# Layer 0's expert tiles: rows stored by one transfer from 32 partitions, rows loaded as two halves

## The reference, cut to what matters

```python
h2 = rms_norm(x, norm2_g) * (1 + sc2) + sh2      # 512 x 1024
gates = top 2 of the best group of 4 experts, per token
for e in range(16):                              # w_gate, w_up: 1024 x 512; w_down: 512 x 1024
    a = silu(h @ w_gate[e]) * (h @ w_up[e])
    out = out + gates[:, e:e + 1] * (a @ w_down[e])
```

## Time and profile before

| what | value |
|---|---|
| runs, us | 980.45, 981.01, 983.0 |
| profiled execution, span, us | 981.6 |
| TensorE busy, share of the span | 85% |
| VectorE / ScalarE / GpSimd busy | 41% / 16% / 15% |
| mean granted clock of TensorE | 0.928 |
| moved by DMA | 322.56 MB, mean 329 GB/s |

### The profile page before, as it was taken

One profiled execution on the slowest core, in us unless ns is written; L12 is line 12 of the kernel. 1 busy time (PEld: TensorE's weight loads), 2 busy tenths in 40 slices (PEclk: granted clock), 3 DMA queues, 4 the chain that ended last, 5 costly groups with the idle time before them and its releaser, 6 DMA issues.

```text
span 981.6 us, 22337 instructions
## 1 busy us (share of the span) xinstructions
PE 830.5 (85%) x8859; PEld 485.7 (49%) x8859; DVE 406.2 (41%) x893; ACT 159.5 (16%) x384; POOL 151.3 (15%) x284
## 2 busy tenths in 40 slices
PE   4699999888996889999896671999887899998674
PEld 2236633555444446657463441587544455654332
DVE  2132722676545423333231124641834655553223
ACT  3201100454013011111010011311512000000001
POOL 2302100001402334433231234000000000000000
PEclk9799999999997799999997886899998899999778
DMA  9999997534998899999999995296076799999995
GB/s 355 348 390 374 349 366 285 230 100 163 382 413 311 338 343 398 391 397 385 384 394 402 399 381 199 89 340 257 1 290 256 293 419 420 420 419 399 418 412 235
DMA packets 82359, 322.56 MB, mean 329 GB/s; under 512 B 10688, under 2 KB 28320, under 8 KB 57712
## 3 DMA queue, kind: packets, MB, share of 16 engines
q1 hardware_dynamic: 62544, 288.42, 75.3%
q0 software_dynamic: 12160, 27.89, 8.0%
q10 hardware_dynamic: 7584, 5.19, 1.8%
HBM read 297.27 MB, written 24.28 MB: 328 GB/s over the span
## 4 chain that ended last, share of the span: by engine, by line
DMA 46%; PE 41%; DVE 7%; issue 3%; ACT 2%; POOL 1%; SPq 0%; DVEq 0%; POOLq 0%; ACTq 0%
DMA weight_ring<-in_w_up_dram 19%; DMA weight_ring<-in_w_gate_dram 18%; PE bank2to L1374 9%; DMA weight_ring<-in_w_mod_dram 5%; PE bank2to L1252 5%; PE bank L1255 4%; PE bank2to L1255 4%; PE bank L1465 4%; PE bank L1252 4%; PE bank2to L1155 2%; DVE score_max L1791 2%; DMA weight_ring<-in_w_in_dram 1%; DMA h_by_expert<-q_k_transposed,slot_numbers 1%; PE bank L1477 1%; PE bank L1327 1%
## 5 line engine op out<-in xcount | busy, mean ns | idle before, releaser
L1465 PE MATMUL bank<-weight_ring,qk_tokens 128*32 128x256 f32 x3824 | 250.9, 406 | 59.5 <-DMA weight_ring<-in_w_up_dram 54.3
L1465 PEld LDWEIGHTS bank<-weight_ring,qk_tokens 128*32 128x32 f32 x3824 | 145.2, 116 | 147.4 <-issue 86.3
L881 POOL DMA_DIRECT2D qk_tokens<-h_by_expert x144 | 71.6, 497 | 161.2 <-DVE qk_tokens L2040 132.3
L1374 PE MATMUL bank2to<-weight_ring 128*128 128x512 f32 x192 | 83.9, 595 | 2.9 <-DVE weight_ring L1819 2.9
L1093 ACT ACTIVATE qk_tokens<-bank 64x256 f32<-64x256 f32 x62 | 23.3, 375 | 374.2 <-PE bank L1465 374.2
L2040 DVE STREAM_TRANSPOSE qk_tokens<-qk_tokens 128x256 f32<-128x256 f32 x36 | 23.6, 655 | 142.6 <-PE bank L1465 132.2
L1477 PE MATMUL bank2to<-weight_ring,qk_tokens 128*32 128x256 f32 x1280 | 79.3, 385 | 1.0 <-DVE qk_tokens L2053 1.0
L818 POOL TENSOR_SCALAR row_stats<-row_stats 128x1 f32<-128x1 f32 x22 | 4.7, 214 | 436.2 <-ACT weight_ring L1136 224.1
L2048 DVE TENSOR_TENSOR qk_tokens<-qk_tokens,bank 64x256 f32<-64x256 f32 x62 | 26.2, 423 | 102.8 <-ACT qk_tokens L1093 101.5
L2053 DVE STREAM_TRANSPOSE qk_tokens<-qk_tokens 64x128 f32<-64x128 f32 x124 | 51.1, 412 | 27.8 <-PE bank2to L1477 26.1
L1477 PEld LDWEIGHTS bank2to<-weight_ring,qk_tokens 128*32 128x32 f32 x1280 | 48.0, 113 | 25.6 <-issue 2.8
(11 more groups left out here) (277 smaller groups left out, 918.3 us busy)
## 6 DMA issues: line engine op xcount, KB each, us to landing
weight_ring<-in_w_down_dram SPq DMA_DIRECT2D x64, 1024.0 KB, 7.6
weight_ring<-in_w_up_dram SPq DMA_DIRECT2D x63, 1024.0 KB, 8.5
weight_ring<-in_w_gate_dram SPq DMA_DIRECT2D x60, 1024.0 KB, 8.4
weight_ring<-in_w_mod_dram SPq DMA_DIRECT2D x24, 2048.0 KB, 10.1
weight_ring<-in_w_in_dram SPq DMA_DIRECT2D x12, 1024.0 KB, 9.1
h_by_expert<-qk_tokens POOLq DMA_DIRECT2D x17, 512.0 KB, 16.4
weight_ring<-in_w_out_dram SPq DMA_DIRECT2D x4, 2048.0 KB, 11.7
y_by_expert<-qk_tokens ACTq DMA_DIRECT2D x158, 32.0 KB, 5.9
```

The source lines that it names most:

```text
L881: pool.dma_start(hrow[i][q * SLOTS:(q + 1) * SLOTS, :], hsort[bass.ds((n * 2 + (AHEAD + i)) * SLOTS, SLOTS), q * Q:(q + 1) * Q]).then_inc( ...
L1374: mm = pe.matmul(pb[2 + n % 2][:, :], mixt(l)[:, k, t * P:(t + 1) * P], wout(l)[:, hf, k, :], start=(k == 0), stop=(k == KD - 1))
L1465: mm = pe.matmul(gate_bank(l)[32 * g:32 * g + 32, 0:Q].rearrange("p (c f) -> p c f", c=2), hTe[:, k * SLOTS:(k + 1) * SLOTS], w.rearrange( ...
```

## The change

Rows of `hsort` hold their four quarters in the order 0, 2, 1, 3, so that one contiguous half of a row holds quarters that belong in partition groups 0 and 2, and the other half those of groups 1 and 3. For that `h2` is written in that order in layer 0 (`rows2` by two VectorE instructions in place of one, then the addition), and TensorE reads its quarters by name (`h2_quarter`).

`hrow[i]` is now 64 partitions by 512 columns, and a tile is loaded by two transfers of 32 rows of 2 KB in place of four of 32 rows of 1 KB. VectorE turns it in two 64x256 steps in place of one 128x256 step. On the way out ScalarE makes four copies of 32x256, one for each quarter, side by side into `yrow[i]` (32 partitions by 1024 columns), and issues one store of 32 rows of 4 KB in place of four of 1 KB. Semaphore counts follow, ScalarE waits once for the zero fill of `hsort` (its source lies under `yrow`), and VectorE no longer waits for an earlier store before it copies out the last tile.

```diff
-        hrow = [qkbuf[:, (4 + i) * Q:(5 + i) * Q] for i in range(2)]
+        hrow = [qkbuf[64 * i:64 * i + 64, 4 * Q:6 * Q] for i in range(2)]
+        yrow = [qkbuf[SLOTS * i:SLOTS * (i + 1), 10 * Q:14 * Q] for i in range(2)]
...
+        def block_of(l, q):
+            return 2 * (q % 2) + q // 2 if l + 1 < DEPTH else q
+        def h2_quarter(l, t, q):
+            return h2[:, t, block_of(l, q) * Q:(block_of(l, q) + 1) * Q]
...
-                        for q in range(AHEAD):
-                            pool.dma_start(hrow[i][q * SLOTS:(q + 1) * SLOTS, :],
-                                           hsort[bass.ds((n * 2 + (AHEAD + i)) * SLOTS, SLOTS), q * Q:(q + 1) * Q]).then_inc(s_hrow[i], 16)
+                        for hf in range(2):
+                            pool.dma_start(hrow[i][hf * SLOTS:(hf + 1) * SLOTS, :],
+                                           hsort[bass.ds((n * 2 + (AHEAD + i)) * SLOTS, SLOTS), hf * MH:(hf + 1) * MH]).then_inc(s_hrow[i], 16)
...
+                act.wait_ge(s_hz, 16 * NZ)
...
-                        act.wait_ge(s_yd[i], stored * 64)
-                    nc.scalar.copy(ysb[i], down_bank(l)[:, 0:Q]).then_inc(s_y[l], 1)
+                        act.wait_ge(s_yd[i], stored * 16)
+                    for q in range(AHEAD):
+                        ins = nc.scalar.copy(yrow[i][:, q * Q:(q + 1) * Q], down_bank(l)[q * SLOTS:(q + 1) * SLOTS, 0:Q])
+                    ins.then_inc(s_y[l], 1)
...
-                    for q in range(AHEAD):
-                        act.dma_start(ysort[tile_rows, q * Q:(q + 1) * Q], ysb[i][q * SLOTS:(q + 1) * SLOTS, :]).then_inc(s_yd[i], 16)
+                    act.dma_start(ysort[tile_rows, :], yrow[i]).then_inc(s_yd[i], 16)
...
-                    link(V.scalar_tensor_tensor(out=h2[:, t, :], in0=xres[:, t, :], scalar=st[:, 3, t:t + 1], in1=scale2(l, s),
-                                                op0=ALU.mult, op1=ALU.mult))
-                    V.tensor_tensor(h2[:, t, :], h2[:, t, :], shift2(l, s), ALU.add).then_inc(s_h2.sem, 1)
+                    for b in range(2):
+                        ins = V.scalar_tensor_tensor(out=h2_columns(l, t)[:, :, b, :], in0=own_order(xres[:, t, :])[:, :, b, :], scalar=st[:, 3, t:t + 1],
+                                                     in1=own_order(scale2(l, s))[:, :, b, :], op0=ALU.mult, op1=ALU.mult)
+                    link(ins)
+                    V.tensor_tensor(h2_columns(l, t), h2_columns(l, t), own_order(shift2(l, s)), ALU.add).then_inc(s_h2.sem, 1)
...
-                    dve.wait_ge(s_hrow[i], loaded * 64)
-                    V.transpose(hTe.rearrange("p (b s) -> p b s", b=KD), in_blocks(hrow[i], KD)).then_inc(s_hT[l], 1)
+                    dve.wait_ge(s_hrow[i], loaded * 32)
+                    for c in range(2):
+                        ins = V.transpose(hTe[64 * c:64 * c + 64, :].rearrange("p (b s) -> p b s", b=KD),
+                                          in_blocks(hrow[i][:, c * Q:(c + 1) * Q], KD))
+                    ins.then_inc(s_hT[l], 1)
...
-                    dve.wait_ge(s_yd[1], pairs * 64 + 64)
```

More of the change, by code:

```diff
@@ L329, in hybrid_trunk, with h2_columns, own_order @@
         place = mt[:, 30:31]
+        def block_of(l, q):
+            return 2 * (q % 2) + q // 2 if l + 1 < DEPTH else q
+        def h2_quarter(l, t, q):
+            return h2[:, t, block_of(l, q) * Q:(block_of(l, q) + 1) * Q]
+        def h2_columns(l, t):
+            return h2[:, t, :].rearrange("p (b a n) -> p a b n" if l + 1 < DEPTH else "p (a b n) -> p a b n", a=2, b=2)
+        def own_order(ap):
+            return ap.rearrange("p (a b n) -> p a b n", a=2, b=2)
         def final_x(t):
@@ L888, in _ @@
                 for i in range(2):
-                    pool.wait_ge(s_yd[i], pairs * 64 + (128 if i == 0 else 96))
+                    pool.wait_ge(s_yd[i], pairs * 16 + (32 if i == 0 else 48))
                 pool.wait_ge(s_yg0, 32)
@@ L1389, in turn_h2 @@
                             kk = 4 * hf + k
-                            mm = pe.transpose(pb[4 + 2 * (t % 2) + hf][:, k * P:(k + 1) * P], h2[:, t, kk * P:(kk + 1) * P], ident)
+                            mm = pe.transpose(pb[4 + 2 * (t % 2) + hf][:, k * P:(k + 1) * P],
+                                              h2_quarter(l, t, kk // 2)[:, (kk % 2) * P:(kk % 2 + 1) * P], ident)
                         mm.then_inc(s_h2p.sem, 1)
@@ L1542, in pick_first @@
                         for j in range(AHEAD):
-                            mm = pe.matmul(pick_bank(T)[32 * j:32 * j + 32, 0:Q], picked[:, t, T * SLOTS:(T + 1) * SLOTS], h2[:, t, j * Q:(j + 1) * Q],
+                            mm = pe.matmul(pick_bank(T)[32 * j:32 * j + 32, 0:Q], picked[:, t, T * SLOTS:(T + 1) * SLOTS], h2_quarter(l, t, j),
                                            start=(t == 0), stop=(t == NT[l] - 1), tile_position=(0, 32 * j))
```

## The result

The changed kernel takes 994.15 us (median of 4 runs, 992.86 to 995.86) beside 980.9 us of the kernel before (4 runs, 980.45 to 983.0): ratio 1.0126, 95% interval 1.0107 to 1.0146, some 12 us slower. Forecast were 976.8 us, range 972.5 to 982.5.

A forecast was written before the change was run, and what follows sets the result against it. Layer 0's mixture was taken to go at the pace of DMA weight transfers, with TensorE nearly full. Terms -4.7 + 0.3 - 1.0 + 1.1 + 0.1 = -4.2 us on the 981.6 us span gave 977.4, as median 976.8; range 972.5 to 982.5.

The forecast's parts named there:

- the -4.7 us: Layer 0's DMA-bound stretch: cheaper row loads and stores on some 34 tiles take 4.7 us off.
- Row packets: Loads and stores of a tile in layer 0: engine time falls from 13.5 to 11.26 us, 2.22 us saved.
- VectorE's pair of 1.31 us: Turn of a tile's rows: two 64x256 steps at 655 ns each, 0.65 us more a tile.
- The step of 5.83: Tile step in layer 0 where weights do not hold it up: from 5.18 to 5.83 us, caught up later.
- SyncE starved by 0.3: Expert 5's weights wait for gate and up of tile 7: 0.3 us on (0 to 0.7).
- The start, -1.0: Tile 4's rows land sooner, so the full DMA stretch begins sooner: 1.0 us off (0 to 2).
- ScalarE and the end, +1.1: Four copies delay the last down, and the turn before the last gate and up adds: 1.1 us on (0.5 to 1.8).
- h2's order, +0.1: Writing h2 by two instructions in place of one, on the path for the last token tile: 0.1 us on.
- D: Rival: one-sided SBUF ports slow row traffic, below about 18 GB/s the kernel gets slower; at half rate 1000 us; 11%.
- E: Rival: layer 0's weights also move faster beside lighter row traffic; half the gap gives 973.5 us; 17%.
- B: Rival: latency of weight landings sets the pace, lighter row packets do not shorten it; 981.8 us; 18%.
- C: Rival: VectorE's pair costs much more, say 1.96 us, making the step 6.5 and the time 982 us; 9%.

The follow-up runs named there:

- turn_split: Kernel before with only the turn of a tile done in two 64x256 VectorE steps: 980.8 us, ratio 0.9962; repeated, 979.97 us, 0.9974.
- loads_all_ports: loads_only with each half load written to every fourth of 128 partitions, output not the reference's: 981.32 us, ratio 0.9997 to the kernel before.
- loads_only: Kernel before with the changed half loads, two-step turn and h2 order, but the old stores: 991.73 us, ratio 1.0093.

## Why the prediction was wrong, step by step

**The bound** was read rightly: weights' transfers, end to end, in both kernels. **The step that failed** is the one behind the -4.7 us: it priced the row packets by their own engine time and held the weights' rate still. Beside it stands a term that the sum did not have, the closing wait. The forecast was -4.2 us and the spans show +9.7. Of these 13.9 us the stretch has 9.3 (forecast -4.7 + 0.3, measured +4.9), the close 4.7 and the start 1.4; the rest takes 1.5 off.

- Row packets: 13.5 to 11.26 us a tile was the sum; measured 6.44 + 5.98 = 12.42. The store came near its price, the load saved nothing: 4 KB to one side took 190 ns, where the kernel with all ports takes 162.
- The weights' rate, taken as given, fell from 24.8 to 24.1 GB/s. On twelve experts' 75.5 MB that is 3045 us of engines against 3138, 93 / 16 = 5.8 us on; the rows give back 34 x 1.1 / 16 = 2.3; the queues' shares together fell from 102.2 to 101.2%, some 2 us. The sum, +5.7, is near the +4.9 measured; forecast -4.7.
- VectorE's pair of 1.31 us: 1.30. The step of 5.83: 5.6 to 5.7 from one gate and up to the next. That it is caught up before the end: so; turn_split showed that it costs nothing and even gains. SyncE starved by 0.3: no, expert 5's gate came at 379.14 for 379.00.
- The start, -1.0: the last landing of tile 4 came 1.0 us sooner (346.25 + 8.11 = 354.36 for 355.35), the gate and up behind it 0.4, and expert 4's stream 0.4 later and not sooner. Mis-sized, since the sooner landing did not lift the stream.
- ScalarE and the end, +1.1: four copies 1.49 us, 0.8 on in the tail.
- h2's order, +0.1: too small to be seen in any run.
- Absent from the sum: GpSimd's closing wait, +4.7. Nothing in the profile's views shows it but the gap between the last row and the span's end, and a change of GpSimd's number of transfers was costed by their issue alone.

**The rivals.** D named the right place to look, where the rows land, and was given 11% for the wrong reason: it was priced on the rows' packets, with a threshold of 18 GB/s or 220 ns that they never reached (20.3 and 22.0 GB/s, 190 and 183 ns), so by its own test it was refuted while its effect was there. "Rows are 13% of DMA time" was an argument about the small stream; what decided was the 88% beside it. Its 1000 us was too much all the same. E, that weights profit from lighter rows, had the coupling and the wrong sign; loads_all_ports shows that going from 24.8 to 26.0 GB/s was there to win by placement. B's sign, landings that stay near 9 us, was nearly met (median for up 9.1, then 9.3), but the weights' packets themselves became slower and its 981.8 us is 12 too low. C doesn't fit: the pair took 1.30 us, the chain is still weights' transfers, and the turn cost nothing.

**What is shown and what is argued.** Shown by runs: the loads carry some nine of the twelve microseconds; where their bytes land changes the weights' pace; the whole store costs some 4 us beside alternating loads; the close follows the number and place of GpSimd's transfers. Argued: that the ports are what makes the place count. Open: where the 3 to 6 us are that neither part shows alone (the changed kernel's stretch is only 0.5 to 1.7 us longer than loads_only's), why quarters of 1 KB rows on one side cost little where halves of 2 KB rows cost 4 us more (row length, width and density in time weren't all told apart), why the two-step turn gains 0.3 to 0.4%, and what rule sets the DRAIN.

## What to carry to other kernels

Where a wide stream sets the pace, price a narrow transfer by what the stream loses, not by its own packets: compare the stream's GB/s per engine and its mean packet before and after. Fewer and longer transfers can lose to more and shorter ones if each lands in few partitions. Spread them over all partitions where the layout lets you; else it is worth trying to issue neighbours in a queue to opposite halves of SBUF. And compare the gap between the last row and the end of the span: it can move by 5 us with the number of transfers that GpSimd issued, the last of which landed some 370 us earlier.

## What the runs showed of the hardware that was not expected

- GpSimd's closing DRAIN took 3.95 us with 230 transfers issued, 9.9 with 158, 9.83 with 302, 8.36 with 230 of which 72 were issued in layer 1, and 4.12 with 230 of which the same 72 were issued in layer 0's loop.
- The same 64 KB half loads cost the weights' packets 334.4 ns on one side, 330.4 on two, 313.5 on every fourth partition; with no rows to move layer 1's take 317 ns. So in that one run the well spread row traffic made the weights' packets no slower.
- A load of 4 KB packets on one side cost the engines 6.44 us a tile in the changed kernel and 6.20 in loads_only, beside 6.44 for one of 2 KB packets on both sides.
- Turning 64x256 takes 0.65 us and 128x256 takes 0.655: at these two shapes the number of partitions does not count, so doubling the instructions cost 0.65 us a tile; and it made the kernel 0.3 to 0.4% faster.
